# Cross-attention as one sequence of steps over all heads

## What is computed

```python
def memory_cross_attention(h, m, wq, wk, wv, wo):        # h (1, 1024, 1024), m (1, 256, 1024)
    q = (h @ wq).reshape(B, S, XATTN_HEADS, XATTN_DH)    # 4 heads of 256
    k = (m @ wk).reshape(B, M, XATTN_HEADS, XATTN_DH)
    v = (m @ wv).reshape(B, M, XATTN_HEADS, XATTN_DH)
    s = jnp.einsum('bqhd,bkhd->bhqk', q, k).astype(jnp.float32) * (XATTN_DH ** -0.5)
    p = jax.nn.softmax(s, axis=-1).astype(v.dtype)
    o = jnp.einsum('bhqk,bkhd->bqhd', p, v).reshape(B, S, D_MODEL)
    return o @ wo
```

## Time and profile before

| | |
|---|---|
| median of 3 runs | 2496.13 us |
| the runs | 2492.68, 2496.13, 2496.66 us |
| the profiled execution | 2492.91 us |
| its span in the profile | 2491.2 us |
| PE, DVE, ACT busy in the span | 92%, 75%, 53% |
| mean granted clock of TensorE | 0.952 |

### The profile page before, as it was taken

The page is one execution under the profiler, slowest core; times in us unless marked ns, Lnnn a source line. Parts: engine busy times, 40 slices in busy tenths (PEclk is TensorE's granted clock), DMA queues, the critical chain, the costliest instruction groups (busy, mean ns, idle before and its releaser), DMA issues.

```text
span 2491.2 us, 43598 instructions
## 1 busy us (share of the span) xinstructions
PE 2283.5 (92%) x15432; PEld 1830.2 (73%) x15433; DVE 1867.2 (75%) x2041; ACT 1319.6 (53%) x1486; POOL 369.0 (15%) x321
## 2 busy tenths in 40 slices
PE   6999995699988988899999999999999999999993
PEld 4889884588855975677777777777777777777772
DVE  4599878624134255889898889888889899989994
ACT  5421354413133034666766666666666666767663
POOL 0000000020000301212222121221212212222121
PEclk7999997699999978999999999999999999999997
DMA  4211310231101015999998898899898999999996
GB/s 146 68 51 52 102 53 18 73 121 38 51 17 30 2 68 205 357 300 326 366 329 291 302 334 300 285 320 330 305 307 300 311 333 343 377 320 352 308 327 204
DMA packets 273680, 543.09 MB, mean 218 GB/s; under 512 B 11372, under 2 KB 45472, under 8 KB 273248
## 3 DMA queue, kind: packets, MB, share of 16 engines
q1 hardware_dynamic: 258064, 492.51, 55.4%
q0 software_dynamic: 13632, 46.54, 7.4%
q10 hardware_dynamic: 1904, 2.90, 0.4%
HBM read 503.24 MB, written 38.67 MB: 218 GB/s over the span
## 4 chain that ended last, share of the span: by engine, by line
PE 67%; DVE 10%; DMA 9%; issue 8%; ACT 4%; SPq 0%; ACTq 0%; DVEq 0%; POOLq 0%; POOL 0%
PE PS L2581 10%; PE PS L2140 10%; PE PS L2582 9%; DMA raw<-in_exp_w_up 8%; PE PS L2584 7%; PE PS L2599 6%; PE PS L2372 4%; PE PS L2470 4%; DVE wlo L1938 3%; PE PS L2573 2%; PE PS L2179 2%; ACT whi L1181 2%; PE PS L2544 2%; PE PS L2432 1%; PE PS L2397 1%
## 5 line engine op out<-in xcount | busy, mean ns | idle before, releaser
L1938 DVE TENSOR_TENSOR wlo<-raw,whi 128x2048 fp32r<-128x2048 f32 x408 | 924.1, 2286 | 111.3 <-ACT whi L1181 103.3
L1181 ACT CAST whi<-raw 128x2048 fp32r<-128x2048 f32 x408 | 772.1, 1912 | 171.5 <-DMA raw<-in_exp_w_up 80.8
L2581 PE MATMUL PS<-whi,xhi 128*128 128x512 f32 x1088 | 452.7, 416 | 5.4 <-DVE wlo L1938 5.4
L2582 PE MATMUL PS<-wlo,xhi 128*128 128x512 f32 x1088 | 426.8, 392 | 0.0
L2584 PE MATMUL PS<-whi,xlo 128*128 128x512 f32 x816 | 321.7, 394 | 0.0
L2581 PEld LDWEIGHTS PS<-whi,xhi 128*128 128x128 f32 x1088 | 206.9, 190 | 51.2 <-DVE wlo L1938 12.1
L2582 PEld LDWEIGHTS PS<-wlo,xhi 128*128 128x128 f32 x1088 | 206.0, 189 | 42.1
L2581 PE MATMUL PS<-whi,hhi 128*128 128x512 f32 x544 | 218.2, 401 | 6.8 <-DVE wlo L1938 3.7
L2582 PE MATMUL PS<-wlo,hhi 128*128 128x512 f32 x544 | 212.3, 390 | 0.0
L2584 PEld LDWEIGHTS PS<-whi,xlo 128*128 128x128 f32 x816 | 154.2, 189 | 34.3
L2584 PE MATMUL PS<-whi,hlo 128*128 128x512 f32 x408 | 159.1, 390 | 0.0
(11 more groups left out here) (398 smaller groups left out, 4348.9 us busy)
## 6 DMA issues: line engine op xcount, KB each, us to landing
raw<-in_exp_w_up SPq DMA_DIRECT2D x272, 1024.0 KB, 9.1
raw<-in_exp_w_down SPq DMA_DIRECT2D x136, 1024.0 KB, 10.5
ring<-in_w_in SPq DMA_DIRECT2D x11, 1024.0 KB, 5.4
xres<-in_x SPq DMA_DIRECT2D x4, 1024.0 KB, 10.2
ring<-in_xattn_wk SPq DMA_DIRECT2D x4, 1024.0 KB, 9.1
ring<-in_xattn_wv SPq DMA_DIRECT2D x4, 1024.0 KB, 6.4
ring<-in_w_out SPq DMA_DIRECT2D x4, 1024.0 KB, 7.1
xres<-in_x SPq DMA_DIRECT2D x1, 4096.0 KB, 19.4
```

What stands on the lines that cost most here:

```text
L1181: nc.scalar.copy(whi[:, chunk_slot(c, NSPL), :], raw[chunk_slot(c, NRAW)][:]).then_inc(s_whi, 1)
L1938: nc.vector.tensor_tensor(wlo[:, chunk_slot(c, NSPL), :], raw[chunk_slot(c, NRAW)][:], whi[:, chunk_slot(c, NSPL), :].bitcast(F), ALU.subtract
L2581: pe.matmul(o, hi[:, k, :], wh, start=k == 0 and bias is None, stop=False)
L2582: pe.matmul(o, hi[:, k, :], wl, start=False, stop=False)
```

## The change

Scores, softmax and turns of all four heads become one sequence of 32 steps, with no break between heads, on PE, ACT and DVE alike. The four parts of a head's outputs are no longer issued together: `value_part(step)` puts part b of head h into step 8h + 10 + b, so between the scores and the turn of the next head's tiles 2 to 5 (the last head's parts come in steps 34 to 37, after its last turn). ACT copies a part to `oxH` in the same step, between the exponential and the `pT` copy. DVE subtracts it in the step after, behind that step's normalisation. A part now waits only for the subtraction of the same part of the head before, where all four waited for all four. DVE normalises each tile one step behind its maximum throughout, where before the last tile of a head was normalised in its own step, so the counts in `scaled_max` and `normalised` change. The instructions and their sizes stay as they are.

```diff
...
-            return 4 * TT * h + (4 * t if t else 2)
+            return 4 * n if n else 2
...
-            return 4 * TT * h + min(4 * t + 6, 4 * TT)
+            return min(4 * n + 6, 4 * N_SC)
+
+        def value_part(step):
+
+            h, b = divmod(step - 10, TT)
+            return (h, b) if step >= 10 and b < 4 else None
...
-            for h in range(XH):
-                for t in range(TT):
-                    n = TT * h + t
-                    act.wait_ge(s_sv, scaled_max(n))
-                    if n >= 4:
-                        act.wait_ge(s_pt, n - 3)
-                    nc.scalar.activation(pr[:, n % 4, :], score_bank(n), ACT.Exp, bias=smx[:, n % 4, 1:2],
-                                         scale=XDH ** -0.5, accum_out=smx[:, n % 4, 2:3]).then_inc(s_pe, 1)
-                    if t >= 2:
-                        xprob_drain(h, t - 2)
-                xprob_drain(h, TT - 2)
-                xprob_drain(h, TT - 1)
-                for b in range(4):
-                    m = 4 * h + b
-                    act.wait_ge(s_av, m + 1)
-                    nc.scalar.copy(oxH[:, 2 * h + b // 2, 512 * (b % 2):512 * (b % 2 + 1)],
-                                   PS[:, 4 + b, :]).then_inc(s_ax, 1)
...
+            for step in range(N_SC + 6):
+                if step < N_SC:
+                    xprob(step)
+                if value_part(step):
+                    xout_hi(*value_part(step))
+                if 2 <= step < N_SC + 2:
+                    xprob_drain(step - 2)
...
+            for step in range(N_SC + 7):
+                if step < N_SC:
+                    scale_maximum(step)
+                if 1 <= step <= N_SC:
+                    normalise(step - 1)
+                if value_part(step - 1):
+                    xout_lo(*value_part(step - 1))
...
+            def head_values(h, b):
+                if b == 0:
+                    pe.wait_ge(s_pc, TT * (h + 1))
                 if h:
-                    pe.wait_ge(s_axl, 4 * h)
-                for b in range(4):
-                    ft, th = b // 2, b % 2
-                    for m in range(MT):
-                        ins = pe.matmul(PS[:, 4 + b, :], vx[:, m, XDH * h + P * ft:XDH * h + P * (ft + 1)],
-                                        pT[:, h % 2, m, 512 * th:512 * (th + 1)], start=(m == 0), stop=(m == 1))
-                    ins.then_inc(s_av, 1)
+                    pe.wait_ge(s_axl, 4 * (h - 1) + b + 1)
+                ft, th = b // 2, b % 2
+                for m in range(MT):
+                    ins = pe.matmul(PS[:, 4 + b, :], vx[:, m, XDH * h + P * ft:XDH * h + P * (ft + 1)],
+                                    pT[:, h % 2, m, 512 * th:512 * (th + 1)], start=(m == 0), stop=(m == 1))
+                ins.then_inc(s_av, 1)
+
+            for step in range(N_SC + 6):
+                if step < N_SC:
+                    score(step)
+                if value_part(step):
+                    head_values(*value_part(step))
+                if 2 <= step < N_SC + 2:
+                    turn_probabilities(step - 2)
```

More of the change, by code:

```diff
@@ L330, in build @@
         fills = [slot_of[:g + 1].count(slot_of[g]) for g in range(len(chunks))]
+        N_SC = XH * TT
         def scaled_max(n):
-            h, t = n // TT, n % TT
-            return 4 * TT * h + (4 * t if t else 2)
+            return 4 * n if n else 2
         def normalised(n):
-            h, t = n // TT, n % TT
-            return 4 * TT * h + min(4 * t + 6, 4 * TT)
+            return min(4 * n + 6, 4 * N_SC)
+        def value_part(step):
+            h, b = divmod(step - 10, TT)
+            return (h, b) if step >= 10 and b < 4 else None
         def score_bank(n):
@@ L1073, in _, with xprob_drain @@
                     split_wq(n // 4 + 2)
-            def xprob_drain(h, t):
-                i = TT * h + t
+            def xprob_drain(i):
+                h, t = i // TT, i % TT
                 act.wait_ge(s_pt, i + 1)
@@ L1090, in _, with xprob, xout_hi @@
             split_wo(0)
-            for h in range(XH):
-                for t in range(TT):
-                    n = TT * h + t
-                    act.wait_ge(s_sv, scaled_max(n))
-                    if n >= 4:
-                        act.wait_ge(s_pt, n - 3)
-                    nc.scalar.activation(pr[:, n % 4, :], score_bank(n), ACT.Exp, bias=smx[:, n % 4, 1:2],
-                                         scale=XDH ** -0.5, accum_out=smx[:, n % 4, 2:3]).then_inc(s_pe, 1)
-                    if t >= 2:
-                        xprob_drain(h, t - 2)
-                xprob_drain(h, TT - 2)
-                xprob_drain(h, TT - 1)
-                for b in range(4):
-                    m = 4 * h + b
-                    act.wait_ge(s_av, m + 1)
-                    nc.scalar.copy(oxH[:, 2 * h + b // 2, 512 * (b % 2):512 * (b % 2 + 1)],
-                                   PS[:, 4 + b, :]).then_inc(s_ax, 1)
+            def xprob(n):
+                act.wait_ge(s_sv, scaled_max(n))
+                if n >= 4:
+                    act.wait_ge(s_pt, n - 3)
+                nc.scalar.activation(pr[:, n % 4, :], score_bank(n), ACT.Exp, bias=smx[:, n % 4, 1:2],
+                                     scale=XDH ** -0.5, accum_out=smx[:, n % 4, 2:3]).then_inc(s_pe, 1)
+            def xout_hi(h, b):
+                act.wait_ge(s_av, 4 * h + b + 1)
+                nc.scalar.copy(oxH[:, 2 * h + b // 2, 512 * (b % 2):512 * (b % 2 + 1)],
+                               PS[:, 4 + b, :]).then_inc(s_ax, 1)
+            for step in range(N_SC + 6):
[5 more added lines that the diff above has]
+                    xprob_drain(step - 2)
             split_wo(1)
@@ L1729, in wo_lo, with xout_lo @@
                                         ALU.subtract).then_inc(s_dlv, 1)
-            def xout_lo(h):
-                for b in range(4):
[L1734 to L1737, removed]
+            def xout_lo(h, b):
+                dve.wait_ge(s_ax, 4 * h + b + 1)
+                k, cols = 2 * h + b // 2, slice(512 * (b % 2), 512 * (b % 2 + 1))
+                nc.vector.tensor_tensor(oxL[:, k, cols], PS[:, 4 + b, :], oxH[:, k, cols].bitcast(F),
+                                        ALU.subtract).then_inc(s_axl, 1)
             wo_lo(0)
@@ L1746, in normalise, with scale_maximum @@
                                         ALU.mult).then_inc(s_sv, 1)
[L1749 to L1765, removed]
+            def scale_maximum(n):
+                dve.wait_ge(s_sc, n + 1)
+                if n >= 4:
+                    dve.wait_ge(s_sv, normalised(n - 4))
+                m = smx[:, n % 4, :]
+                nc.vector.reduce_max(m[:, 0:1], score_bank(n), X).then_inc(s_sv, 1)
+                dve.wait_ge(s_sv, scaled_max(n) - 1)
+                nc.vector.tensor_scalar(m[:, 1:2], m[:, 0:1], -(XDH ** -0.5), None, ALU.mult).then_inc(s_sv, 1)
+            for step in range(N_SC + 7):
[5 more added lines that the diff above has]
+                    xout_lo(*value_part(step - 1))
             wo_lo(1)
@@ L2402, in _ @@
             pe.wait_ge(s_dr["q"], 16)
[L2403 to L2408, removed]
-                    for m in range(MT):
[L2410 to L2426, removed]
-                if h:
-                    pe.wait_ge(s_axl, 4 * h)
-                for b in range(4):
-                    ft, th = b // 2, b % 2
-                    for m in range(MT):
-                        ins = pe.matmul(PS[:, 4 + b, :], vx[:, m, XDH * h + P * ft:XDH * h + P * (ft + 1)],
-                                        pT[:, h % 2, m, 512 * th:512 * (th + 1)], start=(m == 0), stop=(m == 1))
-                    ins.then_inc(s_av, 1)
@@ new lines, in score, with turn_probabilities @@
+            def score(i):
+                h, t = i // TT, i % TT
+                if i >= 3:
+                    pe.wait_ge(s_pe, i - 2)
+                for k in range(2):
+                    ins = pe.matmul(score_bank(i), qxT[:, 2 * h + k, P * t:P * (t + 1)],
+                                    kx[:, 2 * h + k, :], start=(k == 0), stop=(k == 1))
+                ins.then_inc(s_sc, 1)
+            def turn_probabilities(i):
+                pe.wait_ge(s_sv, normalised(i))
+                if i >= 1:
+                    pe.wait_ge(s_pc, i)
+                for m in range(MT):
+                    ins = pe.transpose(PS[:, 3, P * m:P * (m + 1)], pr[:, i % 4, P * m:P * (m + 1)],
+                                       ident[:])
+                ins.then_inc(s_pt, 1)
@@ new lines, in head_values @@
+            def head_values(h, b):
+                if b == 0:
+                    pe.wait_ge(s_pc, TT * (h + 1))
+                if h:
+                    pe.wait_ge(s_axl, 4 * (h - 1) + b + 1)
+                ft, th = b // 2, b % 2
+                for m in range(MT):
+                    ins = pe.matmul(PS[:, 4 + b, :], vx[:, m, XDH * h + P * ft:XDH * h + P * (ft + 1)],
```

(2 more changed lines are left out.)

## The result

| | before | after |
|---|---|---|
| median of the runs | 2496.01 us (4 runs, 2492.68 to 2496.66) | 2474.55 us (4 runs, 2470.34 to 2477.86) |
| profiled execution | 2492.91 us | 2476.59 us |
| its span | 2491.2 us | 2474.8 us |

The ratio is 0.9918, interval 0.9901 to 0.9936: 0.8% faster, 21.5 us by the medians and 16.3 by the two profiled executions. The forecast was 2475, range 2467 to 2487.

What follows compares the result with a forecast made beforehand. No engine was full, so an engine-to-engine chain was taken to bound cross-attention. Heads of 17.4 us against 23.90 start the projection 19.4 us earlier: 2473.5 from the profile, 2476.7 from the median, so 2475, range 2467 to 2487.

Steps and rivals of the forecast that it cites:

- The bound of a value step: Steps holding a value part: PE's own work bounds them, 0.86 + 1.74 + 0.25 = 2.85 us; ACT and DVE hide beneath.
- ACT's wait for the part: New ACT wait in value steps: taken as zero cost; on the path it would cost 1.2 us in 12 steps, 15 us.
- An inner head: From one head's first value part to the next's: 7.1 + 1.74 + 3 x 2.85 = 17.4 us against 23.90.
- The last head: Uncovered by a next head: values from 770.2 at full clock, output projection at 778.7, 19.4 us earlier; other end 1.70 us.
- the sign of a clock at 1.00 up to 777: Check in the new profile: granted clock 1.00 from 711 to 777 us; under 0.9 in the merged part would be wrong.
- the likeliest 19.4: Forecast gain in us: the output projection starts at 778.7 instead of 798.08, with all later work moving up.
- the 2473.5 that the sum gave: Whole kernel, profiled execution: 2492.91 - 19.4 = 2473.5 us; the same sum from the median gives 2476.7.
- The clock rival: Cross-attention: PE's granted clock falls once in every head, four times 1.70 us, leaving 12.6 us gain, 2482; chance 0.09.
- Half clock throughout: Everything after 718.9: PE at 1.2 GHz all through the merged stretch, 31.5 us slower, 2528 from the median; chance 0.04.
- The weight loads: Value steps: loads come out from under the matmuls, 1.64 us each, 19.7 us in 12 steps, so 2496; chance 0.03.
- Nothing was given back: Behind the stage: rival that something keeping its own time gives the gain back, so no change; chance 0.04.

Runs made afterwards that it cites:

- half parts: Half a part in each of eight steps 8h+10 to 8h+17 instead of a part in each of four, against the changed kernel: stage 74.4 us against 80.4.

## Why the prediction was right

**The bound of a value step.** PE's 2.85 us were forecast; 2.80 to 2.90 were measured. ACT's wait for the part costs nothing, as the hidden copies at 721.96 and 722.44 show, and the half parts settle it: work that PE does at its own pace sets the step wherever it exceeds the chain.

**An inner head.** Forecast 17.4, measured 17.55. The first plain step still holds a subtraction, which I hid beneath PE's work; there DVE is the bound (the maximum at 733.04 follows right behind the subtraction of 732.44).

**Where the gain comes from.** Step by step, from 23.90 to 17.55 us a head: stall of four subtractions 1.21, clock 1.69, break between heads 1.97, parts among the steps 1.48. That these add up exactly follows from taking them in this order; taken out of the changed kernel, stall and clock together are about 2.5 in place of 2.90. No rival that gives all to one of them holds.

**The last head.** Here a size was off: I took full clock for its values, since its run-up resembles head 0's, and kept 1.70 us as the other end. The clock fell (771.57, 8.78 us), in two executions of two, so the sign of a clock at 1.00 up to 777 failed. With 1.65 us for it, and the heads 0.3 longer, the forecast of 78.4 us for the stage becomes 80.4, as measured. The total of 16.3 us in the profiled executions is below the likeliest 19.4 for this reason and for a start of the stage 1.1 us later; the 21.5 of the medians lies above it, and that difference between executions was not traced. So it is partly luck that the median of 2474.55 falls on the 2475 forecast; the profiled execution, at 2476.59, lies 3.1 us over the 2473.5 that the sum gave for it.

**The clock rival** thus came true once in four heads, not in each: 1.00 in all three inner heads. **Half clock throughout** did not come: PE at the 1.00 level in 719.8 to 771.5. **The weight loads** stay under the matmuls: a value step has ten of them and takes 2.80 us, where exposed loads would have made it 2.85 + 1.64 = 4.5. The Trainium skill has a sentence that a load overlaps a running matmul only when the row groups differ (TensorE: Matmul & The Clock Gate, Part 3, The mechanism). This trace, with its 2.80 us, does not agree with that sentence taken alone. **Nothing was given back** behind the stage: 1693.0 us against 1693.1.

## What to carry to other kernels

Where no engine is full, work out for each step both the chain's pace and the fullest engine's own work; independent matmuls put into steps whose chain is longer than PE's work are free up to that difference, so spread them evenly (half a part in eight steps beat a part in four by 1.6 us a head). Burst work on a side engine, such as four subtractions in a row, stalls the chain even when that engine has time to spare over the stage. Then look at the ends that no neighbour covers, the start and the last head: with them filled and the parts spread evenly, the stage went from 80.4 to 67.8 us, beside the 17.4 us that the change itself took off.

## What the runs showed of the hardware that was not expected

The fall of the granted clock is not fixed by the instructions ahead of it. With the same rows, PE idle for 2.97 or 2.98 us at the start, it fell in seven executions (to 0.52 to 0.65 in the stretch behind) and stayed at 1.00 in two; the changed kernel itself did the one and the other. With the same run-down in three heads of one execution it fell in one. What decides it is left open. In the four executions in which half parts keep PE busy up to the last values, it did not fall behind the start.
